# x's squares summed by token in four columns and spread by transposes; positions loaded as one row

## What is computed

```python
def rms_norm(x, gain=None):
    xf = x.astype(jnp.float32)
    y = xf * lax.rsqrt(jnp.mean(xf * xf, axis=-1, keepdims=True) + EPS)
    ...
def first_block(x, c, positions, w_ada, b_ada, w_in, ...):
    c_act = jax.nn.silu(c)
    mod = c_act @ w_ada[l] + b_ada[l]
    shift, scale, gate = jnp.split(mod, 3, axis=-1)
    h = rms_norm(x) * (1.0 + scale[:, None, :]) + shift[:, None, :]
    proj = h @ w_in[l]
    ...
    ang = positions.astype(jnp.float32)[..., None] * inv_freq
    cos, sin = jnp.cos(ang), jnp.sin(ang)
```

## Time and profile before

| | us |
|---|---|
| median of 3 runs | 2411.77 |
| lowest, highest | 2411.10, 2413.54 |
| the profiled execution, its time | 2411.39 |
| its span | 2409.6 |
| PE busy | 2382.7 |
| DVE busy | 929.5 |
| ACT busy | 859.1 |
| POOL busy | 1019.2 |

### The profile page before, as it was taken

The page is one execution under the profiler, slowest core; times in us unless marked ns, Lnnn a source line. Parts: engine busy times, 40 slices in busy tenths (PEclk is TensorE's granted clock), DMA queues, the critical chain, the costliest instruction groups (busy, mean ns, idle before and its releaser), DMA issues.

```text
span 2409.6 us, 28360 instructions
## 1 busy us (share of the span) xinstructions
PE 2382.7 (99%) x11112; PEld 1894.8 (79%) x11112; DVE 929.5 (39%) x1501; ACT 859.1 (36%) x1328; POOL 1019.2 (42%) x447
## 2 busy tenths in 40 slices
PE   9999999999999999999999999999999999999997
PEld 5676777778888888887788787878788888888886
DVE  7856465675301700403455443434322413103113
ACT  6465455542323422223343333333333213113322
POOL 5453333344555344443333242434344444444554
PEclk9999999999999999999999999999999999999998
DMA  9962333345444442332223232323333544453332
GB/s 355 401 227 61 119 112 110 110 138 183 149 144 132 137 140 90 97 99 83 80 62 88 71 109 88 110 88 103 94 99 98 166 145 126 131 171 118 89 104 88
DMA packets 100423, 307.94 MB, mean 128 GB/s; under 512 B 10561, under 2 KB 16193, under 8 KB 100289
## 3 DMA queue, kind: packets, MB, share of 16 engines
q1 hardware_dynamic: 100290, 306.13, 39.8%
HBM read 284.06 MB, written 20.97 MB: 127 GB/s over the span
## 4 chain that ended last, share of the span: by engine, by line
PE 90%; DVE 5%; ACT 2%; issue 1%; DMA 1%; SPq 1%; POOL 0%; DVEq 0%; ACTq 0%; POOLq 0%
PE bank L563 25%; PE bank L566 24%; PE bank L564 24%; PE bank L559 2%; PE bank L562 2%; PE bank L560 2%; PE bank L1100 2%; PE bank L1124 2%; PE bank L1112 1%; DVE hlo L1875 1%; PE bank L880 1%; PE bank L891 1%; DVE junk L1933 1%; DVE hlo L2613 1%; DMA rawx<-in_wst 1%
## 5 line engine op out<-in xcount | busy, mean ns | idle before, releaser
L2702 POOL TENSOR_TENSOR wlo<-raw,whi 128x1024 fp32r<-128x1024 f32 x365 | 902.8, 2479 | 1185.8 <-ACT whi L1254 1185.8
L563 PE MATMUL bank<-hhi,whi 128*128 128x512 f32 (+1 forms) x2752 | 1080.6, 393 | 3.4 <-DVE hlo L1956 1.3
L566 PE MATMUL bank<-hhi,wlo 128*128 128x512 f32 (+1 forms) x2752 | 1070.4, 389 | 1.0 <-POOL wlo L2702 1.0
L564 PE MATMUL bank<-hlo,whi 128*128 128x512 f32 (+1 forms) x2752 | 1069.2, 389 | 0.0
L563 PEld LDWEIGHTS bank<-hhi,whi 128*128 128x128 f32 x2752 | 517.4, 188 | 125.8 <-issue 18.3
L566 PEld LDWEIGHTS bank<-hhi,wlo 128*128 128x128 f32 x2752 | 517.2, 188 | 111.8 <-POOL wlo L2702 4.6
L564 PEld LDWEIGHTS bank<-hlo,whi 128*128 128x128 f32 x2752 | 517.6, 188 | 103.8 <-issue 0.7
L1254 ACT ACTIVATE whi<-raw 128x1024 fp32r<-128x1024 f32 x365 | 384.4, 1055 | 587.7 <-PE bank L566 474.5
L2489 DVE TENSOR_SCALAR S<-S,sm 128x512 f32<-128x512 f32 (+1 forms) x64 | 78.0, 1219 | 0.6
L1719 ACT ACTIVATE S<-S,sm 128x512 f32<-128x512 f32 (+1 forms) x64 | 35.3, 551 | 117.3 <-DVE sm L2479 117.3
L562 PE MATMUL bank<-wlo,hhi 128*128 128x512 f32 x192 | 74.8, 390 | 1.0 <-POOL wlo L2702 1.0
(11 more groups left out here) (335 smaller groups left out, 2180.1 us busy)
## 6 DMA issues: line engine op xcount, KB each, us to landing
raw<-in_wst SPq DMA_DIRECT2D x397, 512.0 KB, 3.6
rawx<-in_wst SPq DMA_DIRECT2D x54, 512.0 KB, 9.8
rawy<-in_wst SPq DMA_DIRECT2D x26, 512.0 KB, 4.7
tgs<-TS SPq DMA_DIRECT2D x32, 256.0 KB, 3.8
axr<-tgs SPq DMA_DIRECT2D x32, 256.0 KB, 4.0
X<-in_xt SPq DMA_DIRECT2D x4, 1024.0 KB, 13.1
axr<-in_xt SPq DMA_DIRECT2D x16, 256.0 KB, 2.8
x1s<-X SPq DMA_DIRECT2D x16, 256.0 KB, 2.0
```

Source lines behind the costliest of these rows:

```text
L563: e.matmul(o, hi, xh, start=first, stop=False)
L564: e.matmul(o, hi, xl, start=False, stop=False)
L566: return e.matmul(o, lo, xh, start=False, stop=last)
L2702: e.tensor_tensor(sub(wlo, PAIR[c], CH), slots[slot(c)], sub(whi, PAIR[c], CH).bitcast(F), ALU.subtract).then_inc(*up("wlo_pool", "wlo", c))
```

## The change

The squares of each pair are no longer streamed against all-ones weights. Each 128x128 block of sqs is now the weights, and one column of ones is streamed: 32 matmuls put the sums of the 512 tokens into 128x4 (partition = token within its block, column = block). A matmul of a zero tile, zero4, opens bank 6's accumulation for all four columns. ACT's root and DVE's reciprocal work on these 128x4 (xcol). DVE copies each column 128 times to xb (128x512), and four transposes on PE (`xrow`, a new item of the list before rows(0, 2)) turn it into the form that rsx had. The first two tiles are multiplied straight from the bank, and ACT copies it to rsx for the others. DVE's order changes: reciprocal, copy and the first two rooted tiles come before the scales of (0, 3). On ACT, the copies of blocks 8 and 9 move behind RW and behind the copy to rsx, which waits for the second rooted tile.

The positions are loaded as one row, third in SP's queue, ahead of pt; DVE casts one row, PE spreads it with a matmul of one row of ones after embedding block 1 (bank 5), and DVE reads it there. The first part of the constants now includes ident.

```diff
-           ("xsum", 1), ("ple", 2), *blocks(9), *rows(0, 2), *rows(0, 3), ...
+           ("xsum", 1), ("ple", 2), *blocks(9), ("xrow",), *rows(0, 2), *rows(0, 3), ...
@@ tensor, x_sum
+                    w.wait_ge(*done("zero4"))
+                    e.matmul(o[:, 0:4], C("ones"), zero4, start=True, stop=False)
                 for i in range(4 * half_, 4 * half_ + 4):
                     w.wait_ge(*done("xpair", i))
-                    m = e.matmul(o[:, :], C("ones"), sqs[i][:, :], start=i == 0, stop=i == 7)
+                    for b in range(4):
+                        m = e.matmul(o[:, b:b + 1], sub(sqs[i], b, P), C("ones")[:, 0:1], start=False, stop=i == 7 and b == 3)
+            def x_row():
...
+                w.wait_ge(*done("xb"))
+                for b in range(4):
+                    m = e.transpose(o[:, b * P:(b + 1) * P], sub(xb, b, P), C("ident"))
+            def pos_row():
...
+                w.wait_ge(*done("pf"))
+                e.matmul(o[:, :], one[0:1, :], PF[0:1, :], start=True, stop=True)...
                     embedding(*divmod(item[1], 4))
+                    if item[1] == 1:
+                        pos_row()
@@ scalar
-                    e.activation(rsx[:, :], bank("xsum")[:, :], ACT.Sqrt, scale=1.0 / 2048, bias=epsc)...
+                    e.activation(xcol, bank("xsum")[:, 0:4], ACT.Sqrt, scale=1.0 / 2048, bias=epsc)...
-                elif item == ("pleb", 9):
-                    embedding(range(8, 10))
                 elif item == ("ada", 0, 3):
                     shift_rows(0)
+                    w.wait_ge(*done("xrow"))
+                    w.wait_ge(*done("xr", 1))
+                    e.activation(rsx[:, :], bank("xrow")[:, :], ACT.Copy)...
+                    embedding(range(8, 10))
@@ vector
+            e.memset(zero4, 0.0).then_inc(*up("term_dve", "zero4"))
@@ rooted_x
-                    e.tensor_tensor(sub(X0, k), sub(X0, k), rsx[:, :], ALU.mult)...
+                    e.tensor_tensor(sub(X0, k), sub(X0, k), rsx[:, :] if k > 1 else bank("xrow")[:, :], ALU.mult)...
@@ angles
-                e.tensor_copy(PF[:, :], PI32[:, :])...
+                e.tensor_copy(PF[0:1, :], PI32[0:1, :])...
-                step(PF[:, :], PF[:, :], V("invf"), None, ALU.mult)
+                w.wait_ge(*done("prow"))
+                e.tensor_scalar(PF[:, :], bank("prow")[:, :], V("invf"), None, ALU.mult, ALU.bypass)...
@@ the walk through the list
+            angle_it = angles()
+            next(angle_it)
             decay_terms(True)
...
-                    if (g, j) == (0, 3):
+                    scales(g, j)
+                    if (g, j) == (0, 2):
                         w.wait_ge(*done("xroot"))
-                        e.reciprocal(rsx[:, :], rsx[:, :]).then_inc(*up("norm_dve", "rsx"))
-                    scales(g, j)
-                    if (g, j) == (0, 3):
+                        e.reciprocal(xcol, xcol).then_inc(*up("norm_dve"))
+                        w.wait_ge(*now("norm_dve"))
+                        e.tensor_copy(xb[:, :]..., xcol.unsqueeze(2).to_broadcast([P, 4, P])).then_inc(*up("norm_dve", "xb"))
                         rooted_x(range(2))
+                    elif (g, j) == (0, 3):
                         shifts(0)
@@ sync
+            e.dma_start(PI32[0:1, :], pos).then_inc(*up("pos", by=16))
             e.dma_start(PR[:, :]...
             load(1)
-            e.dma_start(PI32[:, :], pos.to_broadcast([P, NT])).then_inc(*up("pos", by=16))
...
-            first = CST["ident"][0]
+            first = CST["perm"][0]
```

More of the change, by code:

```diff
@@ L59, in opening @@
     out = [("ple", 0), *blocks(1, 2, 3), ("ple", 1), *blocks(5, 6, 7), ("xsum", 0), *rows(0, 0), *rows(0, 1),
-           ("xsum", 1), ("ple", 2), *blocks(9), *rows(0, 2), *rows(0, 3), *blocks(10), ("cols", 0), *blocks(11),
+           ("xsum", 1), ("ple", 2), *blocks(9), ("xrow",), *rows(0, 2), *rows(0, 3), *blocks(10), ("cols", 0), *blocks(11),
            ("ple", 3), *blocks(13, 14, 15)]
@@ L378, in build @@
         rsx = area(48, 1, "rsx")
+        xb = area(50, 1, "xb")
+        xcol = sm[:, 240:244]
+        zero4 = sm[:, 250:254]
         un = [area(50 + 2 * i, 1, f"un{i}") for i in range(4)]
@@ L638, in x_sum @@
                         w.wait_ge(*f)
+                    w.wait_ge("cst", 16)
+                    w.wait_ge(*done("zero4"))
+                    e.matmul(o[:, 0:4], C("ones"), zero4, start=True, stop=False)
                 o = banks[6]
-                w.wait_ge("cst", 16)
                 for i in range(4 * half_, 4 * half_ + 4):
                     w.wait_ge(*done("xpair", i))
-                    m = e.matmul(o[:, :], C("ones"), sqs[i][:, :], start=i == 0, stop=i == 7)
+                    for b in range(4):
+                        m = e.matmul(o[:, b:b + 1], sub(sqs[i], b, P), C("ones")[:, 0:1], start=False, stop=i == 7 and b == 3)
                 if half_:
                     m.then_inc(*up("stat_pe", "xsum"))
+            def x_row():
+                o, prior = claim(6, "xrow")
+                for f in prior:
+                    w.wait_ge(*f)
+                w.wait_ge(*done("xb"))
+                w.wait_ge("cst", 16)
+                for b in range(4):
+                    m = e.transpose(o[:, b * P:(b + 1) * P], sub(xb, b, P), C("ident"))
+                m.then_inc(*up("stat_pe", "xrow"))
+            def pos_row():
+                o, prior = claim(5, "prow")
+                for f in prior:
+                    w.wait_ge(*f)
+                w.wait_ge(*done("pf"))
+                e.matmul(o[:, :], one[0:1, :], PF[0:1, :], start=True, stop=True).then_inc(*up("gate_pe", "prow"))
             def ada_rows(g, j):
@@ L707, in tensor @@
                     x_sum(item[1])
+                elif item[0] == "xrow":
+                    x_row()
                 elif item[0] == "adt":
@@ L1356, in scalar @@
                     w.wait_ge(*done("eps"))
-                    e.activation(rsx[:, :], bank("xsum")[:, :], ACT.Sqrt, scale=1.0 / 2048, bias=epsc).then_inc(
+                    e.activation(xcol, bank("xsum")[:, 0:4], ACT.Sqrt, scale=1.0 / 2048, bias=epsc).then_inc(
                         *up("root_act", "xroot", frees=("xsum",)))
-                elif item == ("pleb", 9):
-                    embedding(range(8, 10))
                 elif item == ("ada", 0, 3):
                     shift_rows(0)
+                    w.wait_ge(*done("xrow"))
+                    w.wait_ge(*done("xr", 1))
+                    e.activation(rsx[:, :], bank("xrow")[:, :], ACT.Copy).then_inc(
+                        *up("root_act", "rsx", frees=("xrow",)))
+                    embedding(range(8, 10))
                 elif item == ("pleb", 10):
@@ L1940, in rooted_x @@
                 for k in ks:
-                    w.wait_ge(*done("rsx"))
+                    w.wait_ge(*(done("rsx") if k > 1 else done("xrow")))
                     w.wait_ge(f"x{k // 4}", 16)
                     w.wait_ge(*done("xsq", k))
-                    e.tensor_tensor(sub(X0, k), sub(X0, k), rsx[:, :], ALU.mult).then_inc(*up("mod_dve", "xr", k))
+                    e.tensor_tensor(sub(X0, k), sub(X0, k), rsx[:, :] if k > 1 else bank("xrow")[:, :], ALU.mult).then_inc(
+                        *up("mod_dve", "xr", k, frees=("xrow",) if k == 1 else None))
             def shifts(g):
@@ L1992, in angles @@
                 w.wait_ge("pos", 16)
-                e.tensor_copy(PF[:, :], PI32[:, :]).then_inc(*up("term_dve", "pf"))
+                e.tensor_copy(PF[0:1, :], PI32[0:1, :]).then_inc(*up("term_dve", "pf"))
                 yield
-                step(PF[:, :], PF[:, :], V("invf"), None, ALU.mult)
+                w.wait_ge(*done("prow"))
+                e.tensor_scalar(PF[:, :], bank("prow")[:, :], V("invf"), None, ALU.mult, ALU.bypass).then_inc(
+                    *up("term_dve", frees=("prow",)))
                 yield
@@ L2027, in vector @@
                 c_rows(i)
-            angle_it = angles()
-            for _ in range(5):
+            for _ in range(4):
                 next(angle_it)
@@ L2033, in vector @@
                     g, j = item[1], item[2]
-                    if (g, j) == (0, 3):
+                    scales(g, j)
+                    if (g, j) == (0, 2):
                         w.wait_ge(*done("xroot"))
-                        e.reciprocal(rsx[:, :], rsx[:, :]).then_inc(*up("norm_dve", "rsx"))
-                    scales(g, j)
-                    if (g, j) == (0, 3):
+                        e.reciprocal(xcol, xcol).then_inc(*up("norm_dve"))
+                        w.wait_ge(*now("norm_dve"))
+                        e.tensor_copy(xb[:, :].rearrange("p (b r) -> p b r", r=P),
+                                      xcol.unsqueeze(2).to_broadcast([P, 4, P])).then_inc(*up("norm_dve", "xb"))
                         rooted_x(range(2))
+                    elif (g, j) == (0, 3):
                         shifts(0)
```

## The result

| | before | after |
|---|---|---|
| median of 14 runs, us | 2412.0 | 2416.92 |
| lowest, highest | 2410.48, 2413.54 | 2415.55, 2419.70 |
| the profiled execution | 2411.39 | 2417.77 |
| its span | 2409.6 | 2416.1 |

A forecast was written before the change was run, and what follows sets the result against it. PE, busy 99% of the span, was taken as the bound. Its +2.1 us of added work against removed waits netted -0.6 to -0.3; taking -0.3, and the profiled run standing 0.4 below the median, gave 2411.5 us, range 2410.0 to 2417.0.

The forecast's parts named there:

- rival 1: One-column x sums in the opening: TensorE's clock falls, +2.4 to +5.9 us, 2413.9 to 2417.4 us; chance 0.32.
- Against: weight loads go on all the time: One-column x sums: argument that the clock would not fall, since the array keeps loading weights; no size given.
- The upper part: Clock falls during or after the first half of the x sums, doubling the second: +5.9 us; half of the 0.32 chance.
- The sum without the clock: Opening up to unit 14: PE's added work +2.1 us against removed waits, net -0.6 to -0.3 us, taken as -0.3.
- four transposes: PE's transposes of xb before rows(0,2): +0.45 us at one record each, +0.9 with two.
- the positions' row: PE's one-row matmul after embedding block 1: +0.9 us, upper end +1.8.
- my 38.9 to 40.1: DVE's chain in the opening: shifts(0) comes between 38.9 and 40.1 us, against 40.42 before.
- the -0.98 for RW: PE's wait for ACT's copy RW, before the first shift columns, disappears: -0.98 us.
- The term for pt: Start of the kernel: the positions' load ahead of pt on SP's queue delays PE, +0.3 us, bounded by 0 and 0.4.
- The ends of the sum's own range: Whole kernel: 2410.2 us with all waits gone and 0.09 us a record, 2413.2 at half-level price with only RW's wait gone.
- Together 2.7 us: all that this change can take from PE's waits: PE's waits in the first 62 us: 1.3 for h's low halves, 0.46 for wlo, 0.98 for RW.
- Rivals 2 and 4: X sums: fresh-tile loads don't overlap, 0.19 us each, 2416.7 us, chance 0.04; transposes wait for xb, 2412.9 us, 0.05.

The follow-up runs named there:

- the pair with one and with 128 columns: Kernel before plus 32 matmuls nobody reads amid wout2's projections, with one column each (2424.36 us) or 128 columns each (2418.25 us).
- the kernel with 128 columns: Changed kernel with 128 columns of ones streamed against each block of squares in place of one, guard matmul 512 columns: 2411.21 us, 1.0002 to before.
- the late copies: Kernel before with only ACT's two copies of blocks 8 and 9 moved behind its copy RW: 2411.26 us, 0.9999 to before.
- the three with idle matmuls: Kernel before plus matmuls nobody reads amid wout2's projections: 32 of one column 2424.36 us, 32 of 128 columns 2418.25, 16 of one column 2415.91.
- sums alone: Changed kernel with the positions' part undone, the one-column sums kept: 2414.85 us, 1.0017 to before.
- one half wide: Changed kernel with one column for the first four tiles of squares, 128 for the second four, guard matmul 512 columns: 2415.01 us, 1.0016 to before.
- 32 and 16 idle ones: Kernel before plus 32 or 16 one-column matmuls nobody reads amid wout2's projections: 2424.36 us (1.0056) and 2415.91 us (1.0022).

## Why the prediction was wrong

- **The forecast was the sum without rival 1, and rival 1 came.** The step that failed is the weighing in the rival's own paragraph: "Against: weight loads go on all the time". Weight loads alone don't keep the clock, as the pair with one and with 128 columns shows: 0.50 against 1.00 at the same loads. No row spoke for the "against", and one spoke against it: PE was busy for 7.2 us on one-row matmuls, each with its load, and the full ones behind still stood 0.43 us apart. That row has few rows of the array in use and 512 columns, not one column, so it was a hint and no proof; I gave the side that came a third of the chance. The Trainium skill, TensorE: Matmul & The Clock Gate, section "Part 1", says that half rate is the default and that activity of the array releases it; the runs agree, with 0.50 at one column and 1.00 at 64 and at 128, where the records are equally busy.
- **The price of rival 1 was right.** I gave +2.4 to +5.9 us and 2413.9 to 2417.4 us; measured are 2416.92, 6.1 us for the clock where it stands alone, and about 5.3 in the opening (the change's loss of 4.9 us, less the 0.35 of the kernel with 128 columns, plus 0.7 for that kernel's guard, whose 512 columns take 0.85 us where four take 0.13). The upper part, the second half doubled plus blocks 8 and 9 at 0.43, is what the trace shows: 6.99 for 3.7, and twelve matmuls at 0.43. The range's end of 2417.0 held this median by 0.1 us, and only since rival 1 had been let into it; the forecast of no change did not hold.
- **The sum without the clock was about right, in part by luck.** With 128 columns and the clock at 1.00 the kernel takes 0.35 us more than before on the same chip; without the 0.7 us of its guard that is 0.4 us less, where I had 0.3 less. The terms: records 0.11 us apart in both halves; four transposes 0.53 us (36.42 to 36.95) for 0.45; the positions' row 1.05 us (15.52 to 16.57) for 0.9; no wait for RW; unit 14 released with a wait of 0.16 and unit 15 with 0.48, at 60.92 and 62.33 us, where I had 61.0 and no more than 0.3. Luck is in the 60.92: in that execution the clock's first rise came 0.9 us sooner than in before, which brings what stands behind it 0.4 us forward (the positions' row at 15.12 and not at 15.52). DVE's shifts came at 40.00, inside my 38.9 to 40.1, but they waited 0.45 us for TensorE's columns, a step that I had not followed. And the -0.98 for RW was a reading of one execution, as the late copies show.
- **The term for pt had nothing under it.** I took +0.3 us for its later place behind the positions' load. ACT began on pt at 5.51 to 6.00 us in the six profiled executions with the new order and at 5.21 to 6.27 in the seven with the old one, and PE's first products began at 10.03 to 10.25 us in both. The term is nothing, and before's 6.27 was the latest of all.
- **The ends of the sum's own range were added up wrongly.** All 2.7 us of waits gone and 0.09 us a record give 2.1 - 1.4 - 2.7 = -2.0 us, 2409.8 and not 2410.2; the half-level price with RW's wait alone gone gives 2.1 + 0.9 - 0.98 = +2.0 us, 2413.8 and not 2413.2. The final range and the sign don't hang on it.
- **"Together 2.7 us: all that this change can take from PE's waits"** was a fair bound and tells little: the waits for RW and for wlo are one wait of 1.4 to 1.6 us that falls at the one place or at the other. In the sum I had followed DVE's chain for the waits at unit 14, and had waved off the one for wlo with ACT's order; it is the same chain.
- **Rivals 2 and 4** did not come: loads of fresh tiles overlap as others do, and xb stood ready 4 us before its transposes, because these were late, not it.

One reading of the cold start needs care. There the granted clock of before reads 1.00 while the records stand 0.43 us apart:

```profile
10.00:15.40 5.40, 5.40 (x13) 3.96 (x13) 4.71 (x6) 5.05 (x9) 2.89 (x2) 1.00 1.05 399
```

So up to the first rise the half level is read from the spacing alone; in the windows shown from later stretches the two agree, 0.43 us at 0.50 and 0.23 us at 1.00. The moment of that rise also differs by itself: from 13.6 to 15.5 us in the five profiled executions with the same work up to there (before, the late copies and the three with idle matmuls). Single starts in the opening compare to about 1 us and no better.

## What to carry to other kernels

A float32 matmul with a fresh 128x128 of weights took the same 0.11 us a record here with 1, 64 or 128 columns. But in each of the five profiled kernels with a stretch of about 3.5 us or more of one-column matmuls (the changed one, sums alone, one half wide, 32 and 16 idle ones) TensorE fell to half its clock, 3.2 to 5.3 us after the stretch began, although its record shows it busy without a gap, and the full matmuls behind pay part of the bill. Stream more columns than are needed: 64 did here, at no cost that the runs can tell; nothing between 1 and 64 was tried. That was surer than dealing the short ones out among full matmuls. Read the granted clock of the stretch before trusting a price taken from a short sample. A wait that is removed in front of a chain which others share is not time saved until the chain itself is shorter.

## What the runs showed that I had not expected

The clock can fall once elsewhere, by itself. In the run with 128 columns and the positions' part undone, TensorE waited 1.71 us for wlo at 842.96 us, behind 14 us of products with 93 columns, and then the clock was at 0.50:

```profile
842.96 0.50 PE L565 MATMUL bank<-wlo,hhi 128*128 128x512 f32 x1 [1.71 <-POOL wlo L2738]
```
```profile
844.00:847.30 3.30, 3.30 (x9) 2.65 (x8) 1.32 (x1) 0.00 (x0) 3.30 (x2) 0.50 1.02 410
```

The kernel before has there:

```profile
844.00:847.30 3.30, 3.30 (x16) 2.69 (x15) 1.47 (x1) 0.00 (x0) 3.30 (x2) 1.00 1.03 421
```

3.3 us at half the clock cost some 1.7 us (half of them, an estimate). The same fall stands in two more of the thirteen profiled executions, those of the late copies (a wait of 1.60 us) and of the 32 idle matmuls with 128 columns (1.71), which were the slowest of their runs. It is not the length of the wait alone: with 64 columns the wait was 1.71 us as well, with 32 idle matmuls of one column 1.59, and the clock stayed at 1.00; in before it was 1.02 and the clock stayed. Nothing was changed in that part of the kernel. The kernel before looks as if it did this too: of its 79 executions beside the experiments, 11 show a mean granted clock of 0.996 and 2412.8 to 2413.6 us, and the other 68 a higher one and, but for one, at most 2412.6; none of the 11 was kept as a trace. So single executions differ by this much for a reason that lies in no changed line, and a profile that is to be compared should be looked at for it first.
